# Placing the probabilities-times-values step later within a round of a hybrid encoder's attention

## What is computed

```python
# prompt: 2048 tokens, 8 heads x 64; memory: 4 heads x 64 into 256 memory tokens
def fox_block(q, k, v, cq, ck, q_pos, k_pos):        # causal, with a forgetting term
    s = einsum('bqhd,bkhd->bhqk', q, k) * HEAD_DIM ** -0.5
    s = s + cq - ck
    p = softmax(where(k_pos <= q_pos, s, -inf))
    return einsum('bhqk,bkhd->bqhd', p, v)
def memory_attention(q, mk, mv):
    p = softmax(einsum('bqhd,bkhd->bhqk', q, mk) * HEAD_DIM ** -0.5)
    return einsum('bhqk,bkhd->bqhd', p, mv)
# x + concat[fox * silu(g), s5 * silu(g), mem * silu(g)] @ w_out
```

## Time and profile before

| | |
|---|---|
| median of 3 runs | 1497.36 us (1488.17 to 1498.31) |
| the profiled execution's own time | 1497.36 us |
| its span, first to last instruction | 1495.6 us |
| PE busy, share of the span | 95% |
| DVE, ACT, POOL busy | 62%, 50%, 20% |
| mean granted TensorE clock | 0.993 |
| attention rounds in the trace | 797 to about 1309 us |

### The profile page before, as it was taken

The page is one execution under the profiler, slowest core; times in us unless marked ns, Lnnn a source line. Parts: engine busy times, 40 slices in busy tenths (PEclk is TensorE's granted clock), DMA queues, the critical chain, the costliest instruction groups (busy, mean ns, idle before and its releaser), DMA issues.

```text
span 1495.6 us, 28755 instructions
## 1 busy us (share of the span) xinstructions
PE 1422.7 (95%) x10222; PEld 1176.3 (79%) x10222; DVE 927.4 (62%) x1938; ACT 743.0 (50%) x1764; POOL 294.9 (20%) x348
## 2 busy tenths in 40 slices
PE   7999999999999988999999999999999999989998
PEld 7998767788777766777777888888888788768887
DVE  3689764781566776655335666766566666566664
ACT  5666422432433553444334766766567678532221
POOL 1111433100043342210001110100000003364542
PEclk9999999999999999999999999999999999989999
DMA  7776699986279587879975864271533702345552
GB/s 221 247 263 217 214 255 255 322 258 189 85 196 321 187 247 227 259 250 287 317 271 140 219 142 96 69 163 41 124 86 65 150 2 65 133 160 184 189 190 78
DMA packets 211374, 276.06 MB, mean 185 GB/s; under 512 B 73697, under 2 KB 147841, under 8 KB 207745
## 3 DMA queue, kind: packets, MB, share of 16 engines
q1 hardware_dynamic: 210192, 274.22, 62.5%
q10 hardware_dynamic: 1040, 0.00, 0.0%
HBM read 186.93 MB, written 86.00 MB: 182 GB/s over the span
## 4 chain that ended last, share of the span: by engine, by line
PE 51%; DVE 7%; issue 4%; ACT 4%; SPq 3%; POOL 2%; DMA 2%; DVEq 0%; ACTq 0%; POOLq 0%
PE in_g L921 12%; PE attn_pv L2459 10%; PE attn_s L2524 7%; PE attn_t L2443 6%; PE attn_s L2424 3%; PE attn_pv L2524 3%; PE attn_s L2427 3%; DVE attn_tops L2730 2%; ACT attn_probs L2557 2%; DVE attn_probs_turned L2743 2%; PE in_b L1096 1%; POOL in_hv L1793 1%; PE in_b L1048 1%; SPq L772 1%; DMA attn_out<-scratch_mem_gate 1%
## 5 line engine op out<-in xcount | busy, mean ns | idle before, releaser
L921 PE MATMUL in_g<-in_wh,in_xh 128*128 128x512 f32 (+2 forms) x904 | 332.6, 381 | 12.0 <-DVE in_z L1532 5.6
L921 PE MATMUL in_g<-in_wl,in_xh 128*128 128x512 f32 (+2 forms) x904 | 322.6, 370 | 0.0
L2730 DVE TENSOR_REDUCE attn_tops<-attn_s 128x1 f32<-128x512 f32 (+3 forms) x288 | 175.3, 617 | 132.8 <-PE attn_s L2427 132.6
L2557 ACT ACTIVATE attn_probs<-attn_s,attn_negmax 128x512 f32<-128x512 f32 (+3 forms) x384 | 227.3, 603 | 32.3 <-DVE attn_negmax L2734 30.8
L921 PE MATMUL in_g<-in_wh,in_xl 128*128 128x512 f32 (+2 forms) x904 | 234.5, 378 | 1.4 <-DVE in_xl L1515 1.3
L2443 PE MATMUL attn_t<-all_ident,attn_probs 128*128 128x128 f32 x1216 | 191.4, 275 | 17.2 <-ACT attn_probs_turned L2567 8.8
L921 PEld LDWEIGHTS in_g<-in_wh,in_xh 128*128 128x128 f32 x904 | 165.8, 189 | 48.9 <-issue 17.7
L2443 PEld LDWEIGHTS attn_t<-all_ident,attn_probs 128*128 128x128 f32 x1216 | 146.5, 141 | 53.7 <-ACT attn_probs L2557 16.8
L921 PEld LDWEIGHTS in_g<-in_wl,in_xh 128*128 128x128 f32 x904 | 165.8, 189 | 28.1
L921 PEld LDWEIGHTS in_g<-in_wh,in_xl 128*128 128x128 f32 x904 | 157.8, 189 | 34.3 <-issue 5.2
L2567 ACT ACTIVATE attn_probs_turned<-attn_t 128x512 f32<-128x512 f32 x168 | 99.1, 590 | 71.6 <-PE attn_t L2443 71.6
(11 more groups left out here) (349 smaller groups left out, 2499.0 us busy)
## 6 DMA issues: line engine op xcount, KB each, us to landing
in_xu<-scratch_xt SPq DMA_DIRECT2D x87, 512.0 KB, 5.3
in_xl<-scratch_xt SPq DMA_DIRECT2D x34, 512.0 KB, 4.8
in_raw<-in_w_in SPq DMA_DIRECT2D x40, 256.0 KB, 5.8
scratch_xt<-in_xu SPq DMA_DIRECT2D x19, 512.0 KB, 5.4
scratch_xt<-in_xl SPq DMA_DIRECT2D x17, 512.0 KB, 6.2
scratch_k<-in_x_turned SPq DMA_DIRECT2D x17, 512.0 KB, 7.1
scratch_q<-in_x_turned SPq DMA_DIRECT2D x17, 512.0 KB, 5.6
in_x_turned<-in_x_prompt SPq DMA_DIRECT2D x16, 512.0 KB, 4.6
```

Source lines behind the costliest of these rows:

```text
L921: last = X.matmul(g_ps[b][:, 0:m], x, ws[:, c, w0:w0 + m], start=(c == 0 and h == 0 and ws is wh), stop=(c == KC - 1 and h == 1))
L2557: last = F(probs[:, s % 2, i, at:at + n, :], s_ps[g % RING][:, at:at + n, :], ACT.Exp, bias=negmax[:, s % 2, top:top + 1], accum_out=total)
L2730: V.tensor_reduce(tops[:, s % 2, i:i + 1], bank[:, 0:n, :].rearrange("p n k -> p (n k)"), AX.X, ALU.max).then_inc(s_top, 1)
```

## The change

In the order list the steps scores (n,1), exp (n-1,3) and turn (n-2,3) are moved ahead of back and values. The step name "copied" goes away: ACT's copy now belongs to the step "values", which follows exp (n-1,3) and turn (n-2,3) as "copied" did. The waits of the copy and of all other steps are the same. PE's order in an iteration with values becomes: scores (n,0), turn (n-2,2), scores (n,1), turn (n-2,3), values, scores (n,2), and on as before; with back in the place of values where there is a back.

```diff
--- before.py
+++ after.py
@@ -1919,16 +1919,13 @@
         some("scores", n, (0,))
         some("exp", n - 1, (2,))
         some("turn", n - 2, (2,))
-
+        some("scores", n, (1,))
+        some("exp", n - 1, (3,))
+        some("turn", n - 2, (3,))
         if n - 4 in last:
             order.append(("back", last[n - 4]))
         if n - 3 in last:
             order.append(("values", last[n - 3]))
-        some("scores", n, (1,))
-        some("exp", n - 1, (3,))
-        some("turn", n - 2, (3,))
-        if n - 3 in last:
-            order.append(("copied", last[n - 3]))
         if first < n <= first + KC:
             order.append(("w_split", n - first - 1, 0))
         some("scores", n, (2,))
@@ -2565,7 +2562,7 @@
 
                         act.wait_ge(s_value, r.group - 1)
                     F(pt[:, r.group % 2, at:at + n, :], t_ps[q % TURNS][:, 0:n, :], ACT.Copy).then_inc(s_read_a, 1)
-                if what == "copied":
+                if what == "values":
                     act.wait_ge(s_value, s + 1)
                     if s:
                         act.wait_ge(s_back, s)
```

## The result

| | before | after |
|---|---|---|
| median of 10 runs | 1493.66 us (1488.17 to 1498.31) | 1501.31 us (1495.80 to 1506.26) |
| the profiled execution's own time | 1497.36 us | 1505.14 us |
| its span | 1495.6 us | 1503.4 us |
| first score of attention to last back step on PE | 511.49 us | 518.96 us |

The ratio is 1.0055, 95% interval 1.0037 to 1.0074: slower by half a per cent. The time lies in the range and inside the 1% that was called no change. By the profiled executions the kernel after is 7.8 us slower. Two of the timed runs further down, one of before at 1785 us and one of B alone at 2792 us, were slow runs and stand in no ratio.

The account below looks back on a forecast made before the run. Attention was taken to run at PE's pace. Added waits less gains made 1.51 us for head 3; head 0 1.1, heads 1 to 6 9.1, head 7 1.3: +11.5 on 1497.36 gave 1509 us, range 1498 to 1518.

Parts of the forecast that it names:

- S(35,2): Score step of bank 2, round 35 (head 3, a round with values): 0.42 us later on PE.
- E(36,0): Exp step of bank 0, round 36 (head 3): 0.61 us later, as DVE's back work stands between score reductions.
- the wait of S(37,1): Score step of bank 1, round 37 (head 3), held before values by round 36's first exp: new wait of 0.87 us.
- The rule S(n,1) = E(n-1,0) + 0.83: In round n, a held score of bank 1 starts 0.83 us after the previous round's exp of bank 0.
- The gain of round 42: Head 3, a round with back: turn 1 of round 41 no longer held by a DVE turn copy, -0.54 us.
- The stall of head 4: Before a turn at 1058.23 us, 2.89 us of issue, then half clock: put at 5 us and called chance.
- the stall goes: Rival: head 4 loses its stall, sum less 5.0, 1504 us; chance 0.13 together with the stall coming once more.
- The bound 1516: Dearer rival: gains in rounds 38 and 42 fail, 0.90 x 7.6 = 6.8 us more, 1516 us; chance 0.18.
- the two gains: Rounds 38 and 42 of head 3: turns no longer held by DVE's turn copies, 0.36 and 0.54 us.
- Faster, 1490: Rival: gains in rounds 38 and 42 win, new waits hidden, 7 us saved, 1490 us; chance 0.08.
- No change, 1497: Rival: each added wait is made good at the next wait for ACT, 1497 us; chance 0.16.
- What would show it: Attention: PE's exp waits from 26 to over 50, 10 to 15 us up; DVE's longest score wait down 0.8 us.

Follow-up runs that it names:

- B alone: Kernel before with only the back step (B) moved behind score (n,1), exp (n-1,3) and turn (n-2,3), values staying ahead of that score: ratio to before 0.9966.
- Scores alone moved: Kernel before with only score (n,1) moved ahead of back and values, exp (n-1,3) and turn (n-2,3) staying behind them: ratio to before 1.0087.
- V alone moved: Kernel before with only the values step (V) moved behind score (n,1), exp (n-1,3) and turn (n-2,3), back staying ahead: ratio to before 1.0054.
- the two kernels with late loads: Kernels before and after, each with head 5's query and key loads started after round 45's last score, not round 43's: ratios to before 0.9983 and 1.0056.
- experiment 5: Kernel before with head 5's query and key loads started after the last score of round 45, not of round 43: ratio to before 0.9983.
- DVE's part of B alone: Kernel before with only DVE's sum, reciprocal and product of the back step moved one reduction and one turn copy later, PE's order unchanged: ratio to before 0.9980.

## Why the prediction was right

The forecast was 1509, the median is 1501.31: inside the range of 1498 to 1518, but below the 1505 that was the lower end of the forecast's own range. Half of the 7.7 us between them is the starting point: the forecast added its 11.5 us to 1497.36, the median of three runs, and the median of ten is 1493.66. The rest is the size by the timed runs, +7.65 us where +11.5 was forecast; 11.5 us is 0.77%, just outside the interval of 0.37 to 0.74%. In the two profiles, with own times of 1505.14 and 1504.46, the mechanism held, step by step. Shifts in head 3 by the timeline (us, PE's unless an exp is named):

| step | predicted | measured |
|---|---|---|
| round 35, S(35,2) | +0.42 | +0.43 |
| round 36, E(36,0) | +0.61 | +0.60 |
| round 37, the wait of S(37,1) | 0.87 | 0.84 |
| round 37, S(37,2) | +1.29 | +1.27 |
| round 38, T(37,1) | +0.93 | +0.94 |
| round 38, E(38,0) | +1.32 | +1.31 |
| round 39, S(39,2) | +1.27 | +1.28 |
| round 41, S(41,2) | +1.67 | +1.72 |
| round 42, T(41,1) | +1.13 | +1.26 |
| round 44, E(44,0) | +1.51 | +1.67 |

- **The rule S(n,1) = E(n-1,0) + 0.83** held to 0.01 us in rounds 35 and 37.
- **The gain of round 42** was too large: 0.54 from between 0.37 and 0.62, measured 0.46. With the 0.05 us more in round 41 the walk of head 3 ends at +1.67 instead of +1.51. Heads 1 to 6 differ, by 1.4 to 1.7 us each, and add 1.54 on average.
- **The sum**, +11.5 in attention; measured 12.3 and 12.4. Head 0 gave 1.2 (1.1), heads 1 to 6 9.2 (9.1; without head 4's stall), head 7 1.9 (1.3).
- **The stall of head 4** was left in, at 5 us. Both profiles of after lack it, which is the rival "the stall goes", 1504: that is where the profiled executions are. It was called chance. Its size does change from execution to execution (2.89 and 0.81 us in the same kernel), but its place doesn't, and it moved when the loads were moved.
- **The bound 1516** rested on a wrong step: if the two gains failed, their 0.9 us a head would be lost on top. Scores alone moved lost them and took +12.0, not more than the kernel after. E(38,0) is late by 1.2 to 1.3 in either case, and whoever arrives earlier waits longer.
- **Faster, 1490**, named the real gain of B's move and priced it at 7 us; alone it is worth 4.5, and 6.1 in the two rounds where it helps. The new waits that it took for hidden are not: V alone moved costs 10.5.
- **No change, 1497**, fell: the waits weren't made good at the next wait for ACT, since the exp moves with PE.
- **What would show it.** Waits for an exp rose to 57, as said, 31 of them right before a V. PE's weight loads wait 19.6 us more, over the 10 to 15; the matmuls, which the weight loads overlap, wait 11.8 us more (6.5 to 18.3). The waits for DVE's turn copies fell from 14 to 1. DVE's longest wait sank by 0.3 us, not 0.8. It is the time from DVE's last work beside V to the first score behind V. That work ends 0.59 us after V's start in before (993.57 - 4.70 = 988.87, V at 988.28) and 0.88 us after it now (999.54 - 4.40 = 995.14, V at 994.26): the score and the turn that DVE has more stand ahead of V on PE too, and V starts that much later.

**What stays open.** The net attention time says +12.3 us, 0.82%. The medians say 0.55% and 0.70%, the two kernels with late loads 0.73% (0.77% by their medians). The first interval (up to 0.74%) leaves that out by a little. A stall that before has in part of its runs and after has not would close this, and its direction fits. But moving it away gave before 2.5 us once, with 0.83 us of it still there in the profile, and nothing the other time, so its share isn't shown. The rest may lie in the 800 us ahead of attention, where executions of one kernel differ by several us.

## What to carry to other kernels

A long step that waits for nobody is cover: see which wait stands behind it before moving that step's successor ahead of it, because the wait comes along, and the engine that starts in order pays it in full. When two engines share an order list, try the move on one engine alone: all of the gain here came from a few short DVE instructions done one reduction and one copy later, none of it from PE's order. And a gain on an engine that next waits for a late exp is no gain; add gains and losses along the walk, not as a list.

## What the runs showed of the hardware

A refill of PE's instructions comes later while data loads run. A 16,384-byte packet of the instruction queue that falls into 14 us of loads on all 16 DMA engines comes 18 to 24 us after the one before it, in the kernels with the loads in their first place, in place of the 8 to 13 us that most have. Six profiles have "issue" time before T(45,0) (2.89, 2.34, 2.02, 0.81, 0.62, 0.50 us); in all six the turn starts 2.7 to 3.0 us after the packet. In the seven with the packet more than 5 us ahead, and in one at 2.80, there is none. A seventh, with late loads, has it in T(47,2), 2.72 us after its packet (experiment 5). The loads alone don't decide it. The packet before that of head 4 in the kernel before, at 1033.59, was itself late with no load running, after 351 instructions of PE in the trace, and the next came after another 432, where a packet brings some 256 (21,302 instructions of PE in all for 83 packets); why that one was late isn't shown, and of heads 1 to 6 only head 3 has one like it. By these counts PE had fewer instructions in hand there when head 5's loads began, which fits that only head 4 stalls.

Of the clock: with the idle time of 2.89 us it fell to 0.50, the 1.2 GHz level, at 1057.65, 0.6 us before the idle time ended, and stayed there for 6.8 us; with 2.02 us it was half for 3.4 us; and with 2.34 us not at all, which the windows show:

```profile
1055.00:1065.00 10.00, 7.30 (x45) 5.57 (x46) 6.32 (x14) 4.92 (x12) 0.00 (x0) 1.00 0.84 176
```

```profile
1056.00:1060.00 4.00, 3.56 (x16) 3.07 (x16) 1.46 (x4) 1.44 (x4) 0.00 (x0) 0.57 1.15 226
```

(B alone moved; DVE's part of B alone; the last three numbers are the granted clock, the DMA share and GB/s.) So an idle time of 2.3 us cost 2.5 us in all, and one of 2.9 us, with the half clock behind it, 4.9. The Trainium skill ("Runtime: NRT & Kernel Launch", Instruction fetch mechanics) says that the sequencer fetches blocks of 256 instructions by its own DMA queue while it executes the current one, and that the cost is mostly hidden. The trace agrees on the queue and the size (83 packets of 256 make 21,248, and the trace has 21,302 instructions of PE, among them 10,222 matmuls and as many weight loads), and "mostly" has its exception here: in heads 1 to 6 of before one refill each came late among the loads, and in head 4 it showed.
